# Mixer of a fused transformer kernel: compressed-block weights spread between other chunks, a third buffer for decayed tokens, exponents in steps 1 and 2, masks ahead of gates

## The chip, the cores and the metric

One core of one Trainium2 chip. The metric is the device time of one execution in microseconds (us). The kernel before took 1908.52 us (median of 3 runs, 1904.62 to 1910.46).

## The reference, cut to what matters

Two transformer blocks on 256 tokens of width 1024, in float32. The first block is FFN, hybrid mixer, FFN; the second holds four more FFNs and two other attention mixers. The change touches the hybrid mixer alone:

```python
o_nsa = nsa_group(...)     # 8 heads: window, selected and compressed-block attention
o_hg  = hgrn2_group(...)   # 4 heads of a gated linear recurrence, chunks of 64 tokens
return jnp.concatenate([o_nsa, o_hg], -1) @ w_out

# hgrn2: f = lb + (1-lb)*sigmoid(z); b = cumsum(log f) in a chunk
decay = jnp.exp(jnp.where(tril, b[t] - b[s], NEG))
a = einsum('bhtd,bhtsd,bhsd->bhts', qc, decay, kc)
o = einsum('bhts,bhsv->bhtv', a, vc) + (qc * exp(b)) @ state
```

The compressed blocks of the attention part are windows of 32 tokens (15 of them), put through a hidden layer of 256 (weights `cmp_w1`, GELU) and a second layer, once for keys and once for values.

## The kernel before, in words

**Weights.** All weights come from memory in 128-partition chunks of up to 1.5 MB, in the order of use, through four buffers `w_raw`; chunk i goes into the buffer that chunk i-4 leaves. SyncE (SP) issues the loads in order, each behind a wait until chunk i-4 is used (`load`, L1815). A chunk is split for exact products at the fast matmul rate: ScalarE (ACT) makes `w_hi` (L319), VectorE (DVE) makes `w_lo` = raw - hi (L326), each with two buffers; TensorE (PE) makes three products per tile (L354 feature-major, L363 token-major). The `cmp_w1` chunks are the exception: they are multiplied raw (L775) and leave their buffer when PE has used them (`hid_tile`).

**Mixer, first part** (`pe_mixer`, L752). PE works through `nsa_a`, `nsa_v`, `hg_g` (2 chunks), `hg_fq` (4), `hg_v` (2), `cmp_w1` (4), `nsa_b`, `nsa_c`. ACT and DVE turn the results into gates, queries, keys and the logarithms of the forget gates; DVE scans them into `b_sum` (L1093).

**Decayed tokens.** Per hgrn head, eight "levels" of exponents are written into a buffer `decayed` of 128 x 2048: DVE's `away(h)` writes differences of `b_sum` (L1106 to L1116), ACT's `decays(h)` takes their exponential (L942), GpSimd's (POOL) `left(h)` multiplies half of it by `hk` (L1229), DVE's `right(h)` the other half by `hq` (L1124). There are two such buffers, lent from `gains` and `logs`. Heads 0 and 1 are made before the steps, heads 2 and 3 inside steps 2 to 5.

**Steps.** Then come STEPS = 8 steps (and two in which the last outputs drain), a loop of k on every engine. Step k takes attention head k and unit k of the recurrence (head k//2, token block k%2). In it, by engine:

- PE: `scores(k)` (L802 to L807), `values(k-2)` (L819 to L821), `level_products(k)` (L831 to L838), `turn_output(k-2)` (L843), `outputs(k-1)` (L850), `turn_weights(k-1)` (L862 to L866).
- DVE: `mean_square(k-2)` (L1139), `weights(k)` (L1154 to L1164: bias and maximum), `gate_output(k-2)` (L1146), `value_lo(k-2)` (L1170), `gated_weights(k)` (L1183 to L1190: waits for ACT's exponentials and scales them), `mask_levels(k)` (L1199), `output_lo(k-2)` (L1177), and in steps 2 and 4 `away`, in 3 and 5 `right`.
- ACT: `weights(k)` (L973, exponentials of the softmax), `value_hi(k-2)` (L980), `copy_cross` (L991), `output_hi(k-2)` (L985), `keep_output(k-1)` (L997, L999), `copy_weights(k-1)` (L1005 to L1007), and `decays` in 2 and 4.
- POOL: the root for `gate_output(k-2)` (L1245), `sum_levels(k)` (L1236 to L1238, sums the masked levels), and `left` in 2 and 4.

The order on each engine is written out by hand, and every engine works its list in order. After the steps the output projection (`w_out1` x2, `w_out2`) runs, then the next FFN. The first half of `w_out1` is split before the steps.

## Time and profile before

| what | value |
|---|---|
| median of 3 runs | 1908.52 us (1904.62 to 1910.46) |
| the profiled execution | 1906.41 us, its span 1905.1 us |
| PE busy | 1772.9 us, 93% of the span |
| DVE, ACT, POOL busy | 55%, 46%, 6% |
| the chain of work that ended last, by engine | PE 82%, DVE 9%, ACT 5% |
| mean granted TensorE clock | 0.962 of full |
| the mixer | about 207 to 442 us of the span |

The span runs from the first to the last instruction; times below are us from its start. A granted clock of 1.00 is 2.4 GHz on TensorE, 0.50 is 1.2 GHz. A row of the timeline reads: start, duration from first to last end, engine, line, operation, output<-inputs, count, and in brackets the idle time before it and what ended it.

### The profile page before, as it was taken

How to read it: one execution, taken by the hardware profiler on the slowest of the kernel's cores; microseconds unless marked ns; L12 is line 12 of the kernel's file. 1: busy time of each engine (PE TensorE's matmuls, PEld its weight loads, DVE VectorE, ACT ScalarE, POOL GpSimd, SP SyncE). 2: the span in 40 equal slices, each digit the busy share in tenths (PEclk: the TensorE clock that was granted, in tenths of full speed). 3: DMA queues.
4: the chain of work that ended last, by engine and by line, in shares of the span. 5: the costliest groups of instructions: out<-in, count | busy, mean ns of one | idle time of the engine just before them, and what ended most of it. 6: DMA issues, size and time to landing. Idle time of an engine off the chain costs nothing.

```text
span 1905.1 us, 28247 instructions
## 1 busy us (share of the span) xinstructions
PE 1772.9 (93%) x11932; PEld 1616.4 (85%) x11932; DVE 1048.9 (55%) x1709; ACT 878.7 (46%) x1507; POOL 107.3 (6%) x147
## 2 busy tenths in 40 slices
PE   7999987789999999989989998899998998999985
PEld 7999987568999999988779998799997776899984
DVE  5555566745455554555755545465556554554555
ACT  5444445435444444445644444454443554444443
POOL 0000003311000000002110000100000000100000
PEclk9999998779999999999999999999998998999998
DMA  8554353004554555434336454255543232555521
GB/s 333 191 187 169 133 194 150 23 33 161 193 185 181 188 181 185 166 133 178 144 121 227 172 195 168 98 195 191 178 185 127 92 114 78 190 187 193 187 90 44
DMA packets 31965, 301.80 MB, mean 158 GB/s; under 512 B 3792, under 2 KB 4320, under 8 KB 5856
## 3 DMA queue, kind: packets, MB, share of 16 engines
q1 hardware_dynamic: 31840, 300.01, 43.1%
q8 instruction: 94, 1.54, 0.3%
q14 instruction: 31, 0.25, 0.0%
HBM read 298.93 MB, written 1.06 MB: 157 GB/s over the span
## 4 chain that ended last, share of the span: by engine, by line
PE 82%; DVE 9%; ACT 5%; issue 2%; POOL 2%; DMA 1%; SPq 0%; DVEq 0%; ACTq 0%; POOLq 0%
PE bank L354 45%; PE bank L363 29%; DVE w_lo L326 2%; ACT w_hi L319 2%; DVE x L584 1%; DVE x L608 1%; PE bank L1276 1%; POOL rstd L668 1%; PE bank L375 1%; DVE xT_lo L617 1%; PE bank L398 1%; PE bank L384 1%; PE bank L399 1%; PE bank L1583 1%; ACT mix_s L973 0%
## 5 line engine op out<-in xcount | busy, mean ns | idle before, releaser
L326 DVE TENSOR_TENSOR w_lo<-w_raw,w_hi 128x1024 fp32r<-128x1024 f32 (+5 forms) x545 | 610.1, 1172 | 398.0 <-ACT w_hi L319 397.4
L319 ACT ACTIVATE w_hi<-w_raw 128x1024 fp32r<-128x1024 f32 (+5 forms) x561 | 525.0, 996 | 290.7 <-PE bank L363 264.2
L354 PE MATMUL bank<-xT_hi,w_hi 128*128 128x256 f32 x2264 | 642.9, 284 | 10.4 <-DVE w_lo L326 9.8
L354 PE MATMUL bank<-xT_hi,w_lo 128*128 128x256 f32 x2264 | 641.5, 283 | 0.0
L354 PE MATMUL bank<-xT_lo,w_hi 128*128 128x256 f32 x2264 | 641.4, 283 | 0.0
L354 PEld LDWEIGHTS bank<-xT_hi,w_hi 128*128 128x128 f32 x2264 | 434.9, 192 | 21.0 <-DVE w_lo L326 11.3
L354 PEld LDWEIGHTS bank<-xT_lo,w_hi 128*128 128x128 f32 x2264 | 434.9, 192 | 4.7
L354 PEld LDWEIGHTS bank<-xT_hi,w_lo 128*128 128x128 f32 x2264 | 434.9, 192 | 0.0
L363 PE MATMUL bank<-w_hi,hT_hi 128*128 128x512 f32 x528 | 207.0, 392 | 0.0
L363 PE MATMUL bank<-w_hi,hT_lo 128*128 128x512 f32 x528 | 206.9, 392 | 0.0
L542 ACT ACTIVATE ff_silu<-bank 128x256 f32<-128x256 f32 x132 | 50.7, 384 | 336.7 <-PE bank L354 334.4
L363 PE MATMUL bank<-w_lo,hT_hi 128*128 128x512 f32 x528 | 205.4, 389 | 0.0
L637 DVE TENSOR_TENSOR ff_silu<-ff_silu,bank 128x256 f32<-128x256 f32 x132 | 55.6, 421 | 185.8 <-ACT ff_silu L542 185.2
L363 PEld LDWEIGHTS bank<-w_lo,hT_hi 128*128 128x128 f32 x528 | 99.2, 188 | 21.7
L363 PEld LDWEIGHTS bank<-w_hi,hT_hi 128*128 128x128 f32 x528 | 99.6, 189 | 17.3
L363 PEld LDWEIGHTS bank<-w_hi,hT_lo 128*128 128x128 f32 x528 | 99.6, 189 | 15.9
L363 PE MATMUL bank<-w_hi,xT_hi 128*128 128x256 f32 (+3 forms) x272 | 93.3, 343 | 9.9 <-DVE xT_lo L617 4.8
L668 POOL TENSOR_TENSOR rstd<-rstd,minus_half 128x1 f32<-128x1 f32 x24 | 21.5, 895 | 1264.2 <-DVE rstd L574 1264.2
L363 PE MATMUL bank<-w_hi,xT_lo 128*128 128x256 f32 (+3 forms) x272 | 92.4, 340 | 0.0
L363 PE MATMUL bank<-w_lo,xT_hi 128*128 128x256 f32 (+3 forms) x272 | 92.0, 338 | 0.0
L639 DVE TENSOR_TENSOR hT_lo<-ff_silu,hT_hi 128x256 fp32r<-128x256 f32 x132 | 56.0, 425 | 63.8 <-ACT hT_hi L546 63.8
L546 ACT ACTIVATE hT_hi<-ff_silu 128x256 fp32r<-128x256 f32 x132 | 55.1, 417 | 64.3 <-DVE ff_silu L637 64.3
(314 smaller groups left out, 2014.4 us busy)
## 6 DMA issues: line engine op xcount, KB each, us to landing
w_raw<-in_ffn_a SPq DMA_DIRECT2D x22, 1536.0 KB, 6.5
w_raw<-in_ffn_b SPq DMA_DIRECT2D x22, 1536.0 KB, 6.4
w_raw<-in_ffn_c SPq DMA_DIRECT2D x22, 1536.0 KB, 6.4
w_raw<-in_ffn_d SPq DMA_DIRECT2D x22, 1536.0 KB, 6.4
w_raw<-in_ffn_e SPq DMA_DIRECT2D x22, 1536.0 KB, 6.4
w_raw<-in_ffn_f SPq DMA_DIRECT2D x22, 1536.0 KB, 6.4
gains<-in_gains SPq DMA_DIRECT2D x11, 1024.0 KB, 4.6
w_raw<-in_mla_up SPq DMA_DIRECT2D x8, 1280.0 KB, 5.7
```

The lines of the kernel that those rows point to most:

```text
L319: nc.scalar.activation(w_hi[c.pair][:, a:b], raw[c.slot][:, a:b], ACTF.Copy).then_inc(w_hi_made, 1)
L326: nc.vector.tensor_tensor(w_lo[c.pair][:, a:b], raw[c.slot][:, a:b], w_hi[c.pair][:, a:b].bitcast(F32), ALU.subtract).then_inc(w_lo_made, 1)
L354: ins = nc.tensor.matmul(o, w[:, c], a[:, k, :], start=(n == 0), stop=(n == last))
L363: ins = nc.tensor.matmul(o, a(k)[:, tok_of(b)], w[:, c], start=(first_k and n == 0), stop=(last_k and n == 3 * len(ks) - 1))
L375: nc.tensor.matmul(psum[7][:, 0:P], ident, ident, start=True, stop=True)
L384: ins = nc.tensor.transpose(bank[:, i * P:(i + 1) * P], src[:, b, (k0 + i) * P:(k0 + i + 1) * P], ident)
L398: nc.tensor.matmul(o, hi[:, c], xT_hi[:, k, :], start=(k == 0), stop=False)
L542: nc.scalar.activation(sig[s][:, :], gate[:, 0:SEQ], ACTF.Silu).then_inc(silu_made, 1)
L546: nc.scalar.activation(hT_hi[s][:, :], sig[s][:, :], ACTF.Copy).then_inc(h_hi_made, 1)
L637: nc.vector.tensor_tensor(sig[s][:, :], sig[s][:, :], up[:, SEQ:2 * SEQ], ALU.mult).then_inc(h_made, 1)
L639: nc.vector.tensor_tensor(hT_lo[s][:, :], sig[s][:, :], hT_hi[s][:, :].bitcast(F32), ALU.subtract).then_inc(h_lo_made, 1)
L668: nc.gpsimd.tensor_tensor(rstd[:, b:b + 1], rstd[:, b:b + 1], expo[:, 0:1], ALU.pow).then_inc(rooted, 1)
```

## The change

1. Stream: the four `cmp_w1` chunks now come ahead of `hg_fq` 2, `hg_fq` 3, `hg_v` 0 and `hg_v` 1, and PE multiplies each right there. Both halves of the hidden layer go to one PSUM bank; the other tiles take other banks. ACT copies `part` and splits `nsa_b` before the two logarithms; DVE splits `nsa_b` ahead of the gain product and the scan.
2. A third buffer for decayed tokens: head 2 uses the `w_raw` buffer of `w_out1` 0 (split before), head 3 uses `gains` again. Loads of `ffn_b` 1 and of the gains wait accordingly.
3. `right(1)` moves into step 0, the split of `w_out1` 0 into steps 0 (ACT) and 1 (DVE), `away(2)` and `away(3)` into steps 1 and 2, their exponents (`decays`) too, `left(2)` and `left(3)` into steps 2 and 3; `right(2)`, `right(3)` stay in 3 and 5. `decays(1)` stands ahead of the copies of the compressed keys (`k_cmp`).
4. In DVE's step `mask_levels(k)` stands ahead of `gated_weights(k)`; in ACT's step `value_hi(k-2)` stands ahead of `weights(k)`.

```diff
+    behind_cmp = {("hg_fq", 2): 0, ("hg_fq", 3): 1, ("hg_v", 0): 2, ("hg_v", 1): 3}
-    for name in ("ffn_a", "nsa_a", "nsa_v", "hg_g", "hg_fq", "hg_v", "cmp_w1", "nsa_b", "nsa_c", "w_out1", "w_out2",
+    for name in ("ffn_a", "nsa_a", "nsa_v", "hg_g", "hg_fq", "hg_v", "nsa_b", "nsa_c", "w_out1", "w_out2",
...
+        for i in range(t[name].shape[0]):
+            if (name, i) in behind_cmp:
+                take("cmp_w1", behind_cmp[name, i])
+            take(name, i)
...
         decayed = [a.rearrange("p (l s) -> p l s", l=LEVELS) for a in (
-            gains[:, 0:LEVELS * SEQ], logs[:, :, :, :].rearrange("p a h s -> p (a h s)"))]
+            gains_lent, logs[:, :, :, :].rearrange("p a h s -> p (a h s)"),
+            raw[chunks[first["w_out1"]].slot][:, 0:LEVELS * SEQ], gains_lent)]
...
+            compressed(0)
+            pe_features(place["hg_fq", 2], [(bank(6), (gate_made_hg, 2)), (bank(7), (gate_made_hg, 3))], mix_tile)
+            compressed(1)
+            pe_features(place["hg_fq", 3], [(bank(0), (gate_made_hg, 4)), (bank(2), (fk_sig_made, 1))], mix_tile)
+            compressed(2)
+            pe_tokens(place["hg_v", 0], SEQ, [(bank(3), (q_made, 1)), (bank(4), (fk_sig_made, 2))], mix_tile)
+            compressed(3)
+            pe_tokens(place["hg_v", 1], SEQ, [(bank(5), (q_made, 2)), (bank(6), (fk_sig_made, 3))], mix_tile)
...
             (act_mixer)
+            act.wait_ge(hid_tile, 4)
+            for kv in range(2):
+                nc.scalar.activation(part[kv], psum[1][:, kv * CMP_HID:(kv + 1) * CMP_HID], ACTF.Copy).then_inc(part_made, 1)
+            act_split(first["nsa_b"])
             flat = lambda a: a.rearrange("p h s -> p (h s)")
             act.wait_ge(floor_made, 1)
...
             copy_values(0)
-            act_split(first["nsa_b"])
-            decays(0)
             copy_values(1)
             act_split(first["nsa_c"])
-            decays(1)
+            decays(0)
...
-            act_split(first["w_out1"])
+            decays(1)
             act.wait_ge(cmp_made, 1)
...
             for k in range(STEPS + 2):
+                if k >= 2:
+                    value_hi(k - 2)
                 if k < STEPS:
                     weights(k)
-                if k >= 2:
-                    value_hi(k - 2)
...
-                if k in (2, 4):
-                    decays(1 + k // 2)
+                if k == 0:
+                    act_split(first["w_out1"])
+                if k in (1, 2):
+                    decays(k + 1)
...
             (dve_mixer)
             away(0)
-            dve_split(first["nsa_b"])
+            dve_split(first["nsa_c"])
+            right(0)
             away(1)
-            right(0)
-            dve_split(first["nsa_c"])
-            right(1)
-            dve_split(first["w_out1"])
...
+                if k == 0:
+                    right(1)
+                elif k == 1:
+                    dve_split(first["w_out1"])
+                    away(2)
+                elif k == 2:
+                    away(3)
+                elif k in (3, 5):
+                    right(2 + k // 5)
                 if k < STEPS:
+                    mask_levels(k)
                     gated_weights(k)
-                    mask_levels(k)
                 if k >= 2:
                     output_lo(k - 2)
-                if k in (2, 4):
-                    away(1 + k // 2)
-                if k in (3, 5):
-                    right(1 + k // 2)
...
             (pool_mixer)
-                if k in (2, 4):
-                    left(1 + k // 2)
+                if k in (2, 3):
+                    left(k)
...
             (sp_program)
-            loads(RAW_SLOTS, first["ffn_b"] + 2)
+            loads(RAW_SLOTS, first["ffn_b"] + 1)
 
             sp.wait_ge(gram_made, 12)
             sp.wait_ge(cross_made, 3)
+            loads(first["ffn_b"] + 1, first["ffn_b"] + 2)
+            sp.wait_ge(gram_made, 16)
+            sp.wait_ge(cross_made, 4)
             load_gains(2)
```

## Rows read from the trace of the kernel before

**Rows 1.** Stretches: us, busy per engine (instructions), granted clock, DMA share, GB/s.

```profile
223.00:280.00 57.00, 56.96 (x506) 55.14 (x504) 36.09 (x64) 29.90 (x54) 0.00 (x0) 1.00 0.51 179
280.00:288.60 8.60, 0.00 (x1) 0.03 (x1) 4.31 (x9) 5.02 (x4) 0.00 (x0) 0.64 1.00 421
...
402.80:417.80 15.00, 10.87 (x35) 6.50 (x35) 2.40 (x9) 3.47 (x11) 3.44 (x5) 0.58 0.00 1
```

**Rows 2.** The chain of waits in order of time, end of the first part.

```profile
277.43 6.10 DMA w_raw<-in_nsa_b
283.55 1.49 ACT w_hi L319
285.07 3.44 DVE w_lo L326 x2
288.60 10.63 PE bank L354 x72
```

**Rows 3.** Timeline of ACT: the second logarithm, and an exponent of a head.

```profile
272.51 1.04 ACT L931 ACTIVATE mix_logs<-mix_logs 128x1024 f32<-128x1024 f32 x1
...
293.04 1.92 ACT L942 ACTIVATE mix_logs<-mix_logs 128x2048 f32<-128x2048 f32 x1 [0.97 <-DVE mix_logs L1116]
```

**Rows 4.** Timeline of DVE: scan, end of `away(0)`, `right(0)` beside POOL, `right(1)` alone.

```profile
274.85 2.44 DVE L1093 TENSOR_TENSOR_SCAN mix_b<-const,mix_logs 128x256 f32<-128x256 f32 x4
...
280.52 0.25 DVE L1116 TENSOR_SCALAR gains<-mix_b 128x64 f32<-128x64 f32 x1
...
292.93 3.77 DVE L1124 TENSOR_TENSOR gains<-gains,xn 128x128 f32<-128x128 f32 x8
...
299.43 2.48 DVE L1124 TENSOR_TENSOR mix_logs<-mix_logs,xn 128x128 f32<-128x128 f32 x8
```

**Rows 5.** Timeline of DVE: where steps 0, 2, 6 and 7 begin, and 7 ends.

```profile
312.76 0.69 DVE L1154 SCALAR_TENSOR_TENSOR mix_s<-const,bank 128x512 f32<-128x512 f32 x1 [1.64 <-PE bank L807]
...
328.31 0.69 DVE L1154 SCALAR_TENSOR_TENSOR mix_s<-const,bank 128x512 f32<-128x512 f32 x1 [0.28 <-PE bank L807]
...
382.71 0.67 DVE L1154 SCALAR_TENSOR_TENSOR mix_s<-const,bank 128x512 f32<-128x512 f32 x1
...
394.03 0.69 DVE L1154 SCALAR_TENSOR_TENSOR mix_s<-const,bank 128x512 f32<-128x512 f32 x1 [2.30 <-PE bank L807]
...
402.77 0.14 DVE L1139 TENSOR_SCALAR mix_rms<-mix_squares 128x1 f32<-128x1 f32 x1
```

**Rows 6.** Timeline of PE: first scores of steps 0, 6 and 7.

```profile
309.41 1.80 PE L802 MATMUL bank<-mix_keys,mix_q 64*128 64x256 f32 x4 [2.62 <-ACT mix_v_cmp L965]
...
378.66 2.07 PE L802 MATMUL bank<-mix_keys,mix_q 64*128 64x256 f32 x4
...
392.06 1.13 PE L802 MATMUL bank<-mix_keys,mix_q 64*128 64x256 f32 x4
```

**Rows 7.** Timeline of DVE, step 0: `gated_weights` from its start to the mask behind it.

```profile
317.53 0.19 DVE L1183 RECIPROCAL mix_sums<-mix_sums 128x6 f32<-128x6 f32 x1 [2.51 <-ACT mix_sc L973]
...
319.13 1.28 DVE L1199 TENSOR_TENSOR lent_x<-bank,const 128x512 f32<-128x512 f32 x2
```

**Rows 8.** Timeline of POOL, step 2: first and last sum of `sum_levels`.

```profile
336.64 1.44 POOL L1236 TENSOR_TENSOR lent_x<-lent_x 128x512 f32<-128x512 f32 x1 [5.46 <-DVE lent_x L1199]
...
339.10 0.59 POOL L1238 TENSOR_TENSOR ff_silu<-lent_x 128x128 f32<-128x128 f32 x1
```

**Rows 9.** Timeline of DVE, step 2: one operation of `away`, beside POOL and alone.

```profile
336.87 1.36 DVE L1108 TENSOR_TENSOR gains<-mix_b 128x128 f32<-128x128 f32 x1
...
340.36 0.28 DVE L1108 TENSOR_TENSOR gains<-mix_b 128x128 f32<-128x128 f32 x1
```

**Rows 10.** Timeline of POOL, step 3: `left(2)`.

```profile
344.00 3.45 POOL L1229 TENSOR_TENSOR gains<-gains,xn 128x128 f32<-128x128 f32 x8 [4.31 <-ACT gains L942]
```

**Rows 11.** Timeline of DVE and of PE, step 3: who waits behind `left(2)`.

```profile
347.99 0.35 DVE L1146 SCALAR_TENSOR_TENSOR mix_o_gated<-mix_o_gated,mix_rms,mix_hg_gate 128x128 f32<-128x128 f32 x1 [3.79 <-POOL mix_rms L1245]
...
348.94 0.45 PE L843 MATMUL bank<-const,mix_o_gated 128*128 128x128 f32 x1 [7.29 <-DVE mix_oT_lo L1170]
```

More of the change, by code:

```diff
@@ L168, in weight_stream @@
                  "ffn_f", "ple1_p", "ple1_g1", "ple1_g2"):
-        first[name] = len(chunks)
-        n, _, cols = t[name].shape
-        for i in range(n):
-            split = cuts(name, i, cols) if name != "cmp_w1" else ()
-            by_pool = 4 if i == 0 and name in ("ffn_b", "ffn_d", "ffn_e", "ffn_f") else 0
-            chunks.append(Chunk(name, t[name][i, :, :], cols, split, by_pool))
+        for i in range(t[name].shape[0]):
+            if (name, i) in behind_cmp:
+                take("cmp_w1", behind_cmp[name, i])
+            take(name, i)
     landed = [0] * RAW_SLOTS
@@ L206, in weight_stream @@
         c.hi_at[j], c.lo_at[j], c.pool_at[j] = hi, lo, pool
-    return chunks, first
+    return chunks, first, place
 FFN = ("ffn_a", "ffn_b", "ffn_c", "ffn_d", "ffn_e", "ffn_f")
@@ L736, in build @@
         LEVELS = 8
+        gains_lent = gains[:, 0:LEVELS * SEQ]
         decayed = [a.rearrange("p (l s) -> p l s", l=LEVELS) for a in (
-            gains[:, 0:LEVELS * SEQ], logs[:, :, :, :].rearrange("p a h s -> p (a h s)"))]
+            gains_lent, logs[:, :, :, :].rearrange("p a h s -> p (a h s)"),
+            raw[chunks[first["w_out1"]].slot][:, 0:LEVELS * SEQ], gains_lent)]
+        fq_and_v = [place["hg_fq", h] for h in range(HG)] + [place["hg_v", 0], place["hg_v", 1]]
         units = [(h, b) for h in range(HG) for b in range(TB)]
@@ L778, in pe_mixer, with compressed @@
-            pe_features(first["nsa_b"], [(bank(7), (fk_sig_made, 4)), (bank(0), (q_made, 4)), (bank(1), (hv_copied, 1))], mix_tile)
+            def compressed(n):
+                kv, half = n // 2, n % 2
+                c = chunks[place["cmp_w1", n]]
+                pe.wait_ge(pads_zeroed, 1)
+                pe.wait_ge(nsa_copied, 2)
+                pe.wait_ge(blocks_made, 4 * kv + 4)
+                pe.wait_ge(w_landed[c.slot], c.landed)
+                for j in range(LP // 2):
+                    lp = half * LP // 2 + j
+                    rows = slice(32 * (lp % 4), 32 * (lp % 4) + N_CMP)
+                    ins = nc.tensor.matmul(psum[1][rows, kv * CMP_HID:(kv + 1) * CMP_HID], blocks[:, kv, lp, :],
+                                           raw[c.slot][:, j * CMP_HID:(j + 1) * CMP_HID], start=(lp < 4), stop=(lp >= LP - 4))
+                ins.then_inc(hid_tile, 1)
@@ L909, in act_mixer @@
                 nc.scalar.activation(vals[:, b, :], psum[3 + b][:, 0:VSW], ACTF.Copy).then_inc(nsa_copied, 1)
-            act_split(first["hg_fq"])
+            act_split(place["hg_fq", 0])
             act.wait_ge(nsa_copied, 5)
@@ L944, in act_mixer @@
             copy_values(0)
-            act_split(first["nsa_b"])
-            decays(0)
             copy_values(1)
             act_split(first["nsa_c"])
-            decays(1)
-            for kv in range(2):
-                act.wait_ge(hid_tile, 2 * kv + 2)
-                nc.scalar.activation(part[kv], psum[5 + kv][:, 0:CMP_HID], ACTF.Copy).then_inc(part_made, 1)
+            decays(0)
             act.wait_ge(mix_tile, 22)
@@ L1057, in dve_mixer @@
             dve_split(first["hg_g"] + 1)
-            dve_split(first["hg_fq"])
+            dve_split(place["hg_fq", 0])
             cmp_gates = gates[:, :, :].rearrange("p b (h three) -> p b h three", three=3)[:, :, :, 0]
@@ L1084, in dve_mixer @@
             nc.vector.tensor_scalar(f, f, LN_RANGE, None, ALU.max).then_inc(floor_made, 1)
+            dve_split(first["nsa_b"])
             by_head = hg[:, :, :].rearrange("p b (h v) -> p (b h) v", v=P)
@@ L1819, in load @@
                 if left >= 0:
-                    name = chunks[left].name
-                    at = left - first[name]
-                    if name == "cmp_w1":
-                        sp.wait_ge(hid_tile, at + 1)
+                    if chunks[left].name == "cmp_w1":
+                        sp.wait_ge(hid_tile, chunks[left].at + 1)
                     else:
```

88 lines of the change are left out of this document (41 added, 47 removed).

## The prediction

> **What bounds the kernel now.** I read the busy time by stretch first. In the first part of the mixer PE is busy all the time at full clock [rows 1]: there the number of matmuls sets the time. Then PE stands still from 280.0 to 288.6. The chain of waits says why [rows 2]: the `nsa_b` load is issued at 277.4, when PE has used the first `cmp_w1` chunk, and takes 6.1 us; ACT's first half of the split (1.5) and DVE's two (3.4) follow. In steps 0 to 7 the starts of DVE's `weights` are the marks [rows 5]: 15.6 us for steps 0 and 1, 54.4 for steps 2 to 5 (four of 13.6), 11.3 for step 6, 8.7 for step 7. Two things hold the long steps. DVE waits 3.8 us for POOL's root, which stands behind `left(2)` [rows 10, 11]. And TensorE's clock falls to 1.2 GHz after its long waits (7.3 us [rows 11]): a whole step of PE, scores to scores, then lasts 13.4 us (378.7 to 392.1), with the same scores at 2.07 us against 1.13 at 2.4 GHz [rows 6]. From 402.8 to 417.8 the last outputs drain, mostly at the lower clock (0.58 granted) [rows 1].
>
> **The change, part by part.** All times are laid on the profiled execution.
>
> *First part.* Each `cmp_w1` chunk costs PE the same wherever it stands (3.7 us for the four, 276.3 to 280.0, by the end of the first part [rows 1, 2]). `nsa_b` now goes into the buffer of the third, used after `hg_fq` 3. PE's order then ends: `hg_fq` 3 at 266.7, third `cmp_w1` 267.7, `hg_v` 0 273.4, fourth 274.4, `hg_v` 1 280.1. So `nsa_b` is issued at 267.7, lands by 274 and stops being on the path. On SP each `hg_fq`/`hg_v` load now stands behind the wait for the `cmp_w1` ahead of it: pairs of 2 MB, issued at 254.4 (`hg_v` 0) and 261.1 (`hg_v` 1). At the 421 GB/s that the engines reached when loads were queued [rows 1] a pair takes 5 us, at the single load's pace [rows 2] 8; they are needed, split, at 267.7 and 274.4, so both fit. ACT waits for the fourth `cmp_w1` (274.4), copies `part` (0.6), splits `nsa_b` (2.9) to 278.0; DVE follows to 280.1. PE goes on at once: the 8.6 us hole closes, and `nsa_b` runs at full clock to 288.9 (it took 10.6 us [rows 2], half as much again as a two-tile chunk of 5.8, so 8.6; 1.9 of it was the clock).
>
> *What is late next.* Behind ACT's wait for `hid_tile` and the split stand the two logarithms: they end at 281.3 instead of 273.5 [rows 3]. DVE's gain product ends then too; sum 1.2, scan 2.4, `away(0)` 3.5 [rows 4] give 288.6 instead of 280.8. The recurrence is 7.8 us later than before, and it is what binds: split of `nsa_c` to 290.8, `right(0)` beside `left(0)` 3.8 [rows 4], `away(1)` to 298.5. `decays(1)` (1.9 [rows 3]) now stands ahead of the `k_cmp` copies: 300.4, copies 300.8, first scores 300.95. PE has been ready since 297.6; that place in ACT's queue costs 3.3 us. The scores began at 309.4 [rows 6]: **8.5 us gained**. `weights(0)` begins at 304.3 for 312.8.
>
> *A step of DVE alone.* `weights` 2.25 (312.76 to the 2.51 us wait that ends at 317.53 [rows 5, 7]), `gate_output` and `value_lo` 0.7, mask 1.2, `gated_weights` 1.6 [rows 7], `output_lo` 0.2: 6.0. Before, 2.5 us of waiting for exponentials came on top [rows 7]; the mask and the earlier `value_hi` now fill that.
>
> *What the new order brings in.* POOL sums the levels right behind the mask, and `gated_weights` now lies beside those sums. Beside the first sum (1.44 us) one DVE operation with two SBUF inputs took 1.36 us instead of its 0.28 [rows 8, 9]: it stood until POOL's ended. The three sums lasted from 336.6 to 339.7. `gated_weights` (six such operations) was never beside POOL in this trace, so I bound it: 1.6 if nothing collides, 1.6 + 3.05 = 4.65 if DVE gets in only when POOL is done. DVE gets a turn between the sums as in [rows 9], so I take 3.7. The Trainium skill (GPSIMD Engine Reference, Specifications) says that POOL's SBUF interfaces are shared with VectorE for instructions with two SBUF inputs. By it `weights`, whose second input is PSUM, is untouched, and `gated_weights` is not. By that rule the masks ahead of the gates give back most of what they win.
>
> *Steps 0 and 1.* Step 0: 2.2 + `right(1)` 2.5 + 1.2 + 3.7 = 9.6. Step 1: 2.2 + split of `w_out1` 3.4 (as large as `nsa_b`'s [rows 2]) + `away(2)` 3.4 + 1.2 + 3.7 = 13.9. Together 23.5 for 15.6: **7.9 lost**. ACT's half of the split hides behind DVE's step 0. PE waits about 5 us in step 1 (314 to 318.9), so I take it at 1.2 GHz until about 334.
>
> *Steps 2 to 5.* Step 2: 6.0 + `away(3)` 3.4 (no POOL beside it) + 2.1 = 11.5. Step 3: POOL sums until 339.0, then `left(2)` 3.45 [rows 10], then the root: DVE waits 1.6; 6.0 + 2.1 + 1.6 + `right(2)` 2.5 = 12.1. Step 4 the same wait behind `left(3)`: 9.7, but PE, at the lower clock after a 3.7 us wait in step 3, gives the levels 0.6 late: 10.3. Step 5: 6.0 + 2.1 + 2.4 = 10.5. Together 44.4 for 54.4: **10.0 gained**.
>
> *Steps 6 and 7.* 8.0 for 11.3, as PE is no longer in its slow stretch: **3.3 gained**. Step 7 8.8 for 8.7. The tail and the projection are taken as before (15.0 and 24.2 us): they hang on PE and on the same chain. Loads of `ffn_b` 1 and the gains wait for levels of steps 5 and 7 (365 and 383) and are needed after 420: nothing. The third buffer itself costs nothing: DVE split its chunk just before.
>
> **Sum:** -8.5 + 7.9 - 10.0 - 3.3 + 0.1 = -13.8. The profiled execution took 1906.4, so 1892.6; the median of the runs shown is 2.1 higher, so 1894.7. I take **1894**.
>
> **The rivals.**
>
> *A. No collision* (chance 0.15). `gated_weights` keeps its 1.6. Each step loses 2.1 less, but in steps without extra work the exponentials (ready 4.8 us into the step) or PE then bind, so I count 1.5 for each of eight: 12 more, **1881**. For it: no row shows this very operation beside POOL. Against: [rows 8, 9].
>
> *B. The gain stays upstream* (0.10). PE at the lower clock in steps 4 to 7, too: each then lasts the 13.4 us of [rows 6]. Against my 10.3, 10.5, 8.0, 8.8 that is +3.1, +2.9, +5.4 and up to +4.6 less what the clock's return takes off: about +9 to +12, **1904** to 1906, no difference that can be measured. Against: full work brought the clock back in the stretch of [rows 6] within one step.
>
> *C. Slower* (0.05). PE's clock decides all steps. If scores(0) to scores(7) take seven times 13.4 = 93.8 us, scores(7) start at 394.8 instead of 392.1 [rows 6], run 3.3 instead of 1.9 us, and values and levels of step 7, at the lower clock, add 4: 8 us late, **1916**. It decides from 13.0 us a step (the 8.5 us upstream, over seven steps, on top of the 11.8 of now). For it: PE's waits of 3 to 5 us in steps 1, 3 and 6 are new or stay.
>
> *D. The loads don't keep up* (0.05). A pair of 2 MB lands after 9 us instead of 5 to 8, and PE waits 2 to 3 us at `hg_v` 0 or 1: **1897**.
>
> **How the numbers follow.** My own case has 0.65. A measurement of this kernel tells 0.3%, 5.7 us, from no change: faster is below 1902.8, slower above 1914.2. Faster: my case, A, D and a small part of B: 0.86. Same: 0.09. Slower: C, 0.05. The range runs from A, 1881, to just short of B's times, 1902: the ends of `gated_weights` (1.6 and 4.65; the upper one adds up to 7.6, 1901.6) lie inside.
>
> **What would show it.** The wait of PE for `nsa_b` gone (right under 1 us, wrong over 3). First scores near 301; over 304 and the recurrence is later than I say. `gated_weights` from its reciprocal to its last product at 3 to 4.6 us and POOL's first sum beside it; at 1.6 it is A. Step 1 the longest of the early ones, 13 to 15 us. DVE's wait for the root in steps 3 and 4, 1 to 3 us, none in 5. Granted clock of steps 2 to 7 above 0.75; at 0.55 it is B or C. Start of the projection at 402 to 406 for 417.8. The times from there to the end must be unchanged; if they aren't, the sum is wrong by what I left out.

## The result, and the profile after

The changed kernel takes **1891.62 us** (median of 4 runs, 1889.33 to 1893.77); the kernel before took 1907.38 beside it. Ratio 0.9912, 95% interval 0.9895 to 0.993: faster by 15.8 us. I had said 1894, in 1881 to 1902. The profiled execution is the quickest of the four (1889.33, span 1888.0).

Stretches of the changed kernel; columns as in [rows 1]:

```profile
223.00:280.00 57.00, 57.00 (x499) 54.14 (x498) 32.57 (x47) 32.01 (x56) 0.00 (x0) 1.00 0.65 240
280.00:301.00 21.00, 16.91 (x142) 16.58 (x142) 16.11 (x52) 13.45 (x20) 8.97 (x11) 1.00 0.49 193
...
336.40:348.80 12.40, 11.56 (x51) 9.20 (x51) 9.96 (x30) 5.07 (x21) 6.95 (x13) 0.63 0.00 1
...
372.00:380.00 8.00, 6.81 (x33) 4.66 (x32) 6.18 (x18) 2.48 (x11) 3.32 (x4) 0.76 0.00 0
...
389.00:404.00 15.00, 11.08 (x54) 7.93 (x54) 5.36 (x8) 5.82 (x12) 0.55 (x1) 1.00 0.07 14
```

PE is busy through 280 and beyond: the second row of [rows 1], 8.6 us without a matmul, has no counterpart. The third row is step 3, mostly at the lower clock. The last row is where the drain ends and the projection begins, at full clock; before, the drain had 0.58. What binds the end of the first part now, by the chain of waits (start, duration, what):

```profile
274.63 2.75 ACT w_hi L327 x2
...
277.40 1.28 ACT L953
...
282.00 2.45 DVE mix_b L1114 x4
...
287.92 2.28 DVE w_lo L334 x2
...
290.29 6.00 PE bank L362 x48
...
296.71 1.28 ACT L965
...
298.01 1.91 ACT mix_logs L965
...
300.29 1.25 PE bank L821 x4
```

Against [rows 2], the load of `nsa_b` is no longer in it. The chain runs through ACT's half of that split, the logarithms (1.28 is the table load ahead of them), the sum, the scan, `away(0)` and the split of `nsa_c`, and at its end through two things on ACT of which I had priced one: the exponent of head 1, and not the load of a function table (1.28) ahead of it.

Where DVE's steps begin and end, and two places inside them (timeline of DVE, for [rows 5, 11]):

```profile
303.10 0.69 DVE L1177 SCALAR_TENSOR_TENSOR mix_s<-const,bank 128x512 f32<-128x512 f32 x1 [6.79 <-PE bank L826]
...
339.70 0.35 DVE L1169 SCALAR_TENSOR_TENSOR mix_o_gated<-mix_o_gated,mix_rms,mix_hg_gate 128x128 f32<-128x128 f32 x1 [1.02 <-POOL mix_rms L1274]
...
381.54 0.69 DVE L1222 TENSOR_TENSOR lent_x<-bank,const 128x512 f32<-128x512 f32 x1 [1.24 <-PE bank L850]
...
387.37 0.14 DVE L1162 TENSOR_SCALAR mix_rms<-mix_squares 128x1 f32<-128x1 f32 x1
```

The wait for POOL's root is 1.02 us (step 3; the same again in step 4) for 3.79 in [rows 11]. Step 7 (from 375.72) became longer: its masks wait for levels that PE makes at the lower clock (0.76 in the window 372 to 380).

`gated_weights` of step 0, timeline of DVE:

```profile
306.88 1.29 DVE L1222 TENSOR_TENSOR lent_x<-bank,const 128x512 f32<-128x512 f32 x2
308.08 0.19 DVE L1206 RECIPROCAL mix_sums<-mix_sums 128x6 f32<-128x6 f32 x1
308.30 1.38 DVE L1210 TENSOR_TENSOR mix_wgt<-mix_sums,mix_gates 128x2 f32<-128x2 f32 x3
309.71 1.76 DVE L1213 TENSOR_TENSOR mix_s<-mix_s,mix_wgt 128x512 f32<-128x512 f32 x2
```

and beside it on POOL:

```profile
308.25 1.27 POOL L1265 TENSOR_TENSOR lent_x<-lent_x 128x512 f32<-128x512 f32 x1 [4.81 <-DVE lent_x L1222]
309.59 0.74 POOL L1266 TENSOR_TENSOR lent_x<-lent_x 128x256 f32<-128x256 f32 x1
```

Three products of 128x2 elements last 1.38 us: as long as POOL's first sum. From the reciprocal's start to the end of the last product it is 3.5 us (308.08 to 311.57), 3.4 to the next operation, where [rows 7] had 1.6.

Where every kernel of this study has its steps, by the start of `weights(k)` on DVE (the last column is the projection's first matmul on PE, us of each span):

| kernel | 0 | 1 | 2 | 3 | 4 | 5 | 6 | 7 | projection | median us |
|---|---|---|---|---|---|---|---|---|---|---|
| before | 312.8 | 320.3 | 328.3 | 342.0 | 355.5 | 369.2 | 382.7 | 394.0 | 417.8 | 1907.4 |
| **changed** | 303.1 | 311.5 | 325.2 | 336.4 | 348.8 | 357.5 | 367.2 | 375.7 | 397.8 | 1891.6 |
| stream_only | 314.4 | 322.0 | 330.0 | 343.6 | 357.2 | 370.9 | 384.4 | 393.6 | 413.9 | 1908.3 |
| old_stream | 312.3 | 320.7 | 334.4 | 345.7 | 357.4 | 366.1 | 377.4 | 386.0 | 408.9 | 1898.1 |
| two_buffers | 303.1 | 311.5 | 321.7 | 332.6 | 345.9 | 356.9 | 370.2 | 381.7 | 403.1 | 1898.3 |
| gates_first | 303.2 | 310.8 | 322.9 | 333.2 | 345.3 | 356.4 | 364.7 | 372.6 | 392.5 | 1887.0 |
| sums_behind | 304.1 | 310.6 | 322.8 | 333.1 | 345.3 | 356.3 | 364.5 | 371.8 | 389.5 | 1882.9 |
| kcmp_first | 299.8 | 309.8 | 323.5 | 334.7 | 347.1 | 355.8 | 367.5 | 376.0 | 399.0 | 1889.0 |
| warm | 304.3 | 312.6 | 326.4 | 337.6 | 348.6 | 357.4 | 367.8 | 376.8 | 400.9 | 1890.1 |
| all3 | 303.5 | 311.7 | 328.8 | 338.0 | 350.2 | 361.1 | 371.4 | 380.6 | 405.7 | 1891.1 |
| sums_kcmp | 301.5 | 309.6 | 321.8 | 332.1 | 344.7 | 355.2 | 363.5 | 370.8 | 390.0 | 1880.7 |
| root_first | 300.0 | 308.2 | 320.3 | 330.7 | 341.1 | 349.0 | 357.8 | 365.3 | 383.0 | **1877.7** |

In the mixer the changed kernel gains 20.0 us up to the projection (417.79 to 397.78), and the projection itself lasts 22.68 for 24.23. Against the projection's start in `before_again`, a second profile of the kernel before, it is 18.2. By the spans the whole kernel gains only 17.1. The rest of the program is the same code; it moved by a few us from one execution to the next (see `before_again`), so I take nothing from it.

### The profile page after: what moved, and what is told of

Its sections match the earlier page's. It is cut to its first block, busy times and chain, and to the rows that moved or that the text cites. A ratio compares the mean times of both kernels' runs of the same rounds, so it can differ in the third digit from the quotient of the medians.

```text
span 1888.0 us, 28249 instructions
## 1 busy us (share of the span) xinstructions
PE 1765.6 (94%) x11932; PEld 1610.1 (85%) x11932; DVE 1052.7 (56%) x1709; ACT 877.5 (46%) x1507; POOL 109.5 (6%) x147
## 4 chain that ended last, share of the span: by engine, by line
PE 82%; DVE 10%; ACT 4%; issue 2%; POOL 1%; DMA 0%; SPq 0%; DVEq 0%; ACTq 0%
PE bank L362 45%; PE bank L371 29%; DVE w_lo L334 2%; ACT w_hi L327 2%; DVE x L592 1%; DVE x L616 1%; PE bank L1305 1%; POOL rstd L676 1%; DVE xT_lo L625 1%; PE bank L406 1%; PE bank L383 1%; PE bank L392 1%; PE bank L407 1%; PE bank L1612 1%; DVE mix_wgt L1210 1%
## 5 line engine op out<-in xcount | busy, mean ns | idle before, releaser
L362 PEld LDWEIGHTS bank<-xT_hi,w_hi 128*128 128x128 f32 x2264 | 434.2, 192 | 13.8 <-issue 5.9
L371 PEld LDWEIGHTS bank<-w_lo,hT_hi 128*128 128x128 f32 x528 | 99.3, 188 | 21.6
```

The costliest lines, as they stand in the source:

```text
L362: ins = nc.tensor.matmul(o, w[:, c], a[:, k, :], start=(n == 0), stop=(n == last))
L371: ins = nc.tensor.matmul(o, a(k)[:, tok_of(b)], w[:, c], start=(first_k and n == 0), stop=(last_k and n == 3 * len(ks) - 1))
```

## The experiments

Each was timed beside the kernel before, on the same chip as it; `before_again` is a single execution. Unless said otherwise the edit is made in the changed kernel. No kernel leaves a part of the computation out.

### Is each part worth something? stream_only, old_stream, two_buffers

**stream_only** keeps part 1 alone: buffers, places of `away`, `right`, `left`, exponents and the orders of a step are those of before.

```diff
             away(0)
-            dve_split(first["nsa_c"])
-            right(0)
             away(1)
+            right(0)
+            dve_split(first["nsa_c"])
+            right(1)
+            dve_split(first["w_out1"])
...
+            decays(0)
             copy_values(1)
             act_split(first["nsa_c"])
-            decays(0)
+            decays(1)
```

> The kernel after with the parts 2, 3 and 4 undone: only the order of the weight chunks and what hangs on it (PSUM banks, nsa_b split ahead of the logarithms) is changed against the kernel before. My theory: PE's wait for nsa_b goes, but the recurrence (logarithms, scan, both away, right(0), split of nsa_c, then ACT's split of w_out1 ahead of the k_cmp copies) is then the bound, and the first scores come only about 1 to 3 us earlier than before (309.4): 1904 to 1907, within 0.3% of the kernel before. Rival (the 8.6 us hole is a gain of its own): 1898 to 1900, first scores near 301.

Measured: 1908.3 us (1904.5 to 1912.14), ratio 1.0005, interval 0.9992 to 1.0017. Within 0.3% of before, as my theory said, though above its 1904 to 1907: the first scores come at 310.8, 1.4 us later than before and not 1 to 3 earlier. The rival (1898 to 1900) fell. Timeline of PE in stream_only:

```profile
300.02 0.55 PE L362 MATMUL bank<-xT_hi,w_hi 128*128 128x256 f32 x1 [9.40 <-DVE w_lo L334]
```

`nsa_b` comes in time, and PE then stands 9.4 us for the split of `nsa_c`, which DVE does last behind the recurrence. The hole of [rows 2] (8.6 us) has moved by one chunk. It is a mechanism that the prediction described ("The recurrence is 7.8 us later than before, and it is what binds"), seen here with DVE's old order behind it.

**old_stream** undoes part 1 and keeps the other three: the four chunks stand together ahead of `nsa_b`, which ACT and DVE split where before did.

```diff
-            if (name, i) in behind_cmp:
-                take("cmp_w1", behind_cmp[name, i])
+            if name == "nsa_b":
+                for n in range(4):
+                    take("cmp_w1", n)
             take(name, i)
```

> The kernel after with part 1 undone: the cmp_w1 chunks stand ahead of nsa_b again, so PE waits for the nsa_b load as before; third buffer, exponents in steps 1 and 2, masks ahead of gates stay. My theory after stream_only (part 1 alone: 1908.3, no gain): the parts need each other. Without part 1 the first scores come at about 306 instead of 300.3 (w_out1's split no longer stands ahead of the k_cmp copies), the steps run as in after: 1896 to 1900. Rival (the gain is in the steps alone, part 1 worth nothing): 1890 to 1893. Other rival (part 1 worth the 8.6 us here): 1900 or more.

Measured: 1898.12 us (1895.08 to 1909.53), ratio 0.9954 (0.9938 to 0.997); inside the theory's 1896 to 1900, though the first scores come at 308.7 and not at 306. The hole is back in front of `nsa_b`; timeline of PE in old_stream:

```profile
287.60 0.55 PE L363 MATMUL bank<-xT_hi,w_hi 128*128 128x256 f32 x1 [8.55 <-DVE w_lo L335]
```

So part 1 is worth 6.5 us by the medians (1898.1 against 1891.6; 11.1 by the projection's start) with the others, and nothing alone. Old_stream also puts the split of `nsa_c` back behind `right(0)` and `away(1)`, where stream_only has it too. PE's wait in stream_only points at that split as what part 1 needs beside it; the split was not moved alone, so this is argued and not shown.

**two_buffers** gives back the two buffers and the late heads: `away`, exponent and `left` of heads 2 and 3 in steps 2 and 4, behind the step's other work, `right` in 3 and 5.

```diff
-            raw[chunks[first["w_out1"]].slot][:, 0:LEVELS * SEQ], gains_lent)]
+            gains_lent, logs[:, :, :, :].rearrange("p a h s -> p (a h s)"))]
...
-                if k in (1, 2):
-                    decays(k + 1)
+                if k in (2, 4):
+                    decays(1 + k // 2)
...
-                if k in (2, 3):
-                    left(k)
+                if k in (2, 4):
+                    left(1 + k // 2)
```

> The changed kernel with two buffers for decayed tokens again: away, exponent and left of heads 2 and 3 in steps 2 and 4, behind the step's other work, right in 3 and 5, all as before; the stream, the places of right(1) and of w_out1's split, and the order of masks and gates stay as in the changed kernel. Theory: the third buffer and the earlier exponents are worth the stall behind left(2) and left(3): the root comes 3 to 4 us late in steps 3 and 5, where it is 1.0 in the changed kernel, while step 1 gets shorter by away(2) (3.4 us). weights(1) to weights(2) about 10.3, steps 2 to 5 together about 48 to 50 instead of 42; 1895 to 1900. Rival: DVE has the same work in either order and the waits overlap with PE's own slow stretches, so the third buffer is worth under 3 us: 1888 to 1894. Another rival: the stall comes whole in both steps and PE's clock falls with it: 1901 or more.

Measured: 1898.34 us (1897.01 to 1902.34), ratio 0.9951 (0.9938 to 0.9963). The theory held. Steps 2 to 5 last 48.6 us (321.7 to 370.2; 42.0 in the changed kernel). Timeline of POOL, step 3 of two_buffers:

```profile
334.63 3.45 POOL L1253 TENSOR_TENSOR gains<-gains,xn 128x128 f32<-128x128 f32 x8 [5.96 <-ACT gains L965]
338.04 0.55 POOL L1269 TENSOR_TENSOR mix_rms<-mix_rms,minus_half 128x1 f32<-128x1 f32 x1
```

and of DVE, steps 3 and 5:

```profile
338.62 0.35 DVE L1165 SCALAR_TENSOR_TENSOR mix_o_gated<-mix_o_gated,mix_rms,mix_hg_gate 128x128 f32<-128x128 f32 x1 [3.79 <-POOL mix_rms L1269]
...
362.92 0.35 DVE L1165 SCALAR_TENSOR_TENSOR mix_o_gated<-mix_o_gated,mix_rms,mix_hg_gate 128x128 f32<-128x128 f32 x1 [3.79 <-POOL mix_rms L1269]
```

`left(2)` waits 5.96 us for its exponent, and DVE then 3.79 for the root: the stall of [rows 10, 11], to the hundredth, back in both steps. The third buffer, with the earlier heads that it allows, is worth 6.7 us by the medians (5.3 by the projection's start).

### The order within a step: gates_first, sums_behind

**gates_first** puts `gated_weights` ahead of `mask_levels` on DVE again, and nothing else.

```diff
                 if k < STEPS:
-                    mask_levels(k)
                     gated_weights(k)
+                    mask_levels(k)
```

> The kernel after with gated_weights(k) ahead of mask_levels(k) again on DVE, nothing else. My theory: the sums on POOL no longer collide with the products (gated_weights back from 3.4 to 1.6 us), but DVE waits for the exponentials again, so the two cancel: within 3 us of the kernel after (1891.6). Rival (the order of masks and gates is worth its full 1.3 us a step): 8 to 12 us slower than after, 1900 to 1904. Other rival (the collision outweighs): up to 6 us faster.

Measured: 1887.01 us (1883.38 to 1892.74), ratio 0.9894 (0.9876 to 0.9912): 4.6 us faster by the medians than with the change's order. The two intervals still overlap (0.9895 to 0.9912), but the trace says the same: the projection starts 5.3 us earlier (392.45 for 397.78). That is the rival in which the collision outweighs what the masks hide. The exponents were not much to hide: DVE waits for them 0 to 1.27 us in this kernel, not the 2.51 of [rows 7]; in the early steps `right(1)`, `away` and the split now fill that time.

By step the picture is less simple. Steps 0, 1, 2 and 5 are 0.8 to 1.5 us shorter. In steps 3 and 4 DVE waits 4.24 us for the root instead of 1.02, since POOL's sums begin later; step 4 is 2.4 us longer. The largest single gain is step 7 with 3.4 us (8.3 for 11.7), and there PE's granted clock is 0.98 where the changed kernel has 0.71. Without step 7 the gain up to the projection would be about 2 us (an estimate from these rows), which is the theory's "within 3 us".

**sums_behind** leaves the masks first and makes POOL's sums wait for `gated_weights`.

```diff
                 pool.wait_ge(masked_made, 2 * u + 2)
+                pool.wait_ge(p_made, u + 1)
                 pool.wait_ge(hg_out_made, u - 1)
```

> The kernel after, where POOL's sum_levels(k) also waits until gated_weights(k) is done (p_made). Same work, no collision. My theory: gated_weights takes 1.6 us instead of 3.4 in each step, DVE's steps shorten where DVE is the bound; in steps 2 and 3 the left multiplications and the root behind the sums are not later than now. 4 to 10 us faster than after: 1882 to 1888. Rival (the collision costs nothing on the path, since exponentials or PE bind the step anyway): 1890 to 1893.

Measured: 1882.87 us (1878.08 to 1890.46), ratio 0.9875 (0.9856 to 0.9895): 8.7 us faster than the changed kernel. A wait was added, and the kernel became faster. Step 0 on DVE:

```profile
309.03 0.18 DVE L1206 RECIPROCAL mix_sums<-mix_sums 128x6 f32<-128x6 f32 x1
309.24 0.30 DVE L1210 TENSOR_TENSOR mix_wgt<-mix_sums,mix_gates 128x2 f32<-128x2 f32 x3
309.58 1.03 DVE L1213 TENSOR_TENSOR mix_s<-mix_s,mix_wgt 128x512 f32<-128x512 f32 x2
```

and the first sum on POOL:

```profile
310.85 1.27 POOL L1266 TENSOR_TENSOR lent_x<-lent_x 128x512 f32<-128x512 f32 x1 [5.76 <-DVE mix_sc L1213]
```

with `weights(1)` beside it on DVE:

```profile
310.62 0.68 DVE L1177 SCALAR_TENSOR_TENSOR mix_s<-const,bank 128x512 f32<-128x512 f32 x1
```

The same three products that took 1.38 us beside POOL take 0.30, and `gated_weights` is back at 1.6. Steps 0 to 2 are shorter by 1.8, 1.5 and 0.9 us, steps 5 and 6 by 1.5 and 1.2. Step 4 is longer (10.9 for 8.7): DVE waits 4.30 us for the root there and in step 3, since POOL now does sums, `left` and root one after the other and starts later.

The largest gain is again step 7, 6.7 us for 11.7, with the granted clock at 1.00 for 0.71. The same order of step 7 as in the changed kernel lasts 8.5 us in two_buffers, at a granted clock of 1.00. So some 3 us of the 8.7 came with PE's clock in step 7 and not from the products themselves (an estimate: 11.7 less 8.5). The clock of step 7 is 0.68 to 0.71 in the changed kernel, kcmp_first and old_stream, and 0.98 or more in gates_first, sums_behind, sums_kcmp and root_first; whether the order brings this about was not tried.

### The end of the first part, and the clock: kcmp_first, warm, all3

**kcmp_first** moves the exponent of head 1 behind the copies of the compressed keys.

```diff
-            decays(1)
             act.wait_ge(cmp_made, 1)
             nc.scalar.activation(k_cmp[:, :], psum[3][:, P:P + GROUPS * NB], ACTF.Copy)
...
+            decays(1)
```

> The kernel after, where ACT copies k_cmp and v_cmp ahead of decays(1) instead of behind it. My theory: decays(1) stands 3.2 us in the way of the first scores (300.3), which then come near 297.5, 1 to 3 us gained in all, as right(1) in step 0 now waits a little for decays(1): 1889 to 1891. Rival (step 0 is bound by the recurrence, so nothing moves): 1891.6 within 1 us.

Measured: 1888.97 us (1883.67 to 1892.76), ratio 0.9902 (0.9884 to 0.992). The first scores come at 297.9 for 300.3, as expected; but step 0 is then 9.9 us for 8.4, since `right(1)` now lies beside `left(1)` and takes 3.25 us instead of 1.70, and the projection starts no earlier (399.0 for 397.8). Its median is 2.6 us lower than the changed kernel's, but the intervals overlap, and the trace does not show the gain behind step 1. I count it as small or nothing.

**warm** keeps PE busy where it waits: matmuls of 128x128 into bank 3, which nothing reads before it is written anew (30 in step 1 ahead of `turn_weights(0)`, 8 to 20 ahead of the values of steps 3 to 8; each is two instructions in the trace).

```diff
+            def warm_step(count):
+                for _ in range(count):
+                    nc.tensor.matmul(psum[3][:, 0:P], ident, ident, start=True, stop=True)
...
                 if k >= 2:
+                    pe.wait_ge(pT_made, 3 * (k - 2) + 3)
+                    warm_step({3: 20, 4: 8, 5: 8, 6: 8, 7: 8, 8: 16}.get(k, 0))
                     values(k - 2)
...
                     outputs(k - 1)
+                    warm_step({1: 30}.get(k, 0))
                     turn_weights(k - 1)
```

> The kernel after with extra 128x128 matmuls into an unused PSUM region where PE waits in steps 1 and 3 to 8 (30, 20, then 8 to 16 of them), so that TensorE's clock stays at 2.4 GHz; they leave the output alone. My theory: in after PE at 1.2 GHz makes DVE wait for the levels in steps 3 and 7 and slows outputs; 4 to 8 us less: 1884 to 1888, granted clock in the steps 0.95 or more for 0.82. Rival (DVE is the bound, clock off the path): 1890 to 1893.

Measured: 1890.14 us (1886.54 to 1892.09), ratio 0.9902 (0.9885 to 0.9919). The time is that of the rival (1890 to 1893) and not of the theory (1884 to 1888). The stretch 300 to 400 in warm:

```profile
300.00:400.00 100.00, 86.58 (x604) 74.43 (x604) 77.11 (x213) 46.25 (x170) 37.19 (x56) 0.97 0.07 27
```

and in the changed kernel:

```profile
300.00:400.00 100.00, 77.09 (x418) 61.80 (x419) 78.83 (x215) 47.36 (x171) 37.13 (x56) 0.83 0.07 27
```

The granted clock rises from 0.83 to 0.97. That the time did not follow is not because the clock is off the path. Steps 3 and 7 and the drain in warm:

```profile
337.60:348.60 11.00, 9.63 (x67) 8.02 (x67) 9.78 (x29) 4.91 (x21) 6.86 (x13) 1.00 0.01 1
...
376.80:386.00 9.20, 7.21 (x52) 5.76 (x51) 7.52 (x20) 4.91 (x21) 3.33 (x4) 0.99 0.31 113
386.00:400.90 14.90, 10.97 (x65) 8.54 (x63) 2.43 (x9) 3.49 (x11) 1.10 (x2) 0.89 0.00 1
```

and what PE does at the start of that drain:

```profile
385.38 5.47 PE L892 MATMUL bank<-const 128*128 128x128 f32 x32 [1.20 <-ACT lent_x L1032]
390.77 0.65 PE L838 MATMUL bank<-lent_x,mix_vals 128*64 128x256 f32 x2
```

Step 3 lasts 11.0 us for 12.3 and step 7 9.2 for 11.7: there the theory had put DVE's waits for PE, and there the clock gave 3.8 us. Steps 5 and 6 became 0.7 and 0.5 longer, but the eight steps together are 2.5 us shorter (81.8 for 84.3). The drain then lasts 14.8 us for 10.4: the values of head 6 stand behind the 16 dummies of step 8 until 390.8. So the dummies took back what the clock had won. Without those of step 8 the kernel would come to about 1885.7 (an estimate: 1890.1 less the 4.4 us of the drain), inside the theory's range; that kernel was not run. The first scores were also 1.9 us later than in the changed kernel (302.2), ahead of any dummy.

**all3** is sums_behind, kcmp_first and warm together.

> The kernel after with three edits together: POOL's sums wait until gated_weights is done, k_cmp copied ahead of decays(1), and the extra matmuls of warm. If the three gains add (8.7 from the sums, 2.6 from k_cmp, 4 to 8 from the clock): 1872 to 1877. If the sums' gain was mostly the better clock it happened to bring, less: 1878 to 1881.

Measured: 1891.07 us (1888.56 to 1897.63), ratio 0.992 (0.9901 to 0.9938). A miss by over 10 us: two edits that gained and a third that had cost no time alone came to nothing together. Timeline of DVE, start of step 2 of all3:

```profile
328.82 0.69 DVE L1184 SCALAR_TENSOR_TENSOR mix_s<-const,bank 128x512 f32<-128x512 f32 x1 [4.87 <-PE bank L826]
```

and of PE ahead of it:

```profile
316.56 9.49 PE L892 MATMUL bank<-const 128*128 128x128 f32 x60
```

PE waits for the later sum ahead of `outputs(0)`, and only then come the 30 dummy matmuls, in front of `turn_weights(0)` and `scores(2)`. In warm they began at 312.7 and took 6.9 us, most of it in a wait (4.8 us in the changed kernel) and without making step 2 later; here the wait had moved ahead of them, and they stood in the way. The drain, with its 16 dummies, lasts 16.4 us, for 12.6 in sums_kcmp below.

### What follows: sums_kcmp, root_first

**sums_kcmp** is all3 without the dummies (the two diffs above).

> The changed kernel with two of its orders altered, as in sums_behind (POOL's sums of a step wait for gated_weights, so that the two don't lie beside each other) and kcmp_first (the copies of the compressed keys ahead of the exponent of head 1), without the dummy matmuls of warm. Theory: the third combination lost because of the 30 dummy matmuls in front of turn_weights(0); without them the two gains (8.7 and 2.6 us alone) add up in part. First scores near 298, step 0 about 9 us long (right(1) waits for the exponent), weights(1) near 309 and every later step as in sums_behind: 1878 to 1882. Rival: step 0 takes back all that kcmp_first gives (weights(1) at 310.6 as in sums_behind): 1882 to 1885. Another rival: outputs(0), late behind the later sum, holds PE in step 1 whatever the dummies do, so weights(2) comes after 325 instead of 322.8: 1886 to 1891.

Measured: 1880.7 us (1879.5 to 1883.73), ratio 0.9858 (0.9841 to 0.9875), within the theory's 1878 to 1882. That the dummies were all3's fault is shown by this pair: 10.4 us between them, and `weights(2)` at 321.8 instead of 328.8. Against sums_behind (1882.9) it is 2.2 us, with overlapping intervals: not a difference that can be counted on. What is left to take is in DVE's steps 3 and 4:

```profile
338.65 0.35 DVE L1169 SCALAR_TENSOR_TENSOR mix_o_gated<-mix_o_gated,mix_rms,mix_hg_gate 128x128 f32<-128x128 f32 x1 [4.28 <-POOL mix_rms L1275]
...
350.82 0.35 DVE L1169 SCALAR_TENSOR_TENSOR mix_o_gated<-mix_o_gated,mix_rms,mix_hg_gate 128x128 f32<-128x128 f32 x1 [3.91 <-POOL mix_rms L1275]
```

**root_first** moves `left(2)` and `left(3)` behind the root of the next step on POOL.

```diff
                     pool.wait_ge(ms_made, k - 1)
                     nc.gpsimd.tensor_tensor(rms[k % 2][:, :], rms[k % 2][:, :], expo[:, 0:1], ALU.pow).then_inc(ms_rooted, 1)
+                if k in (3, 4):
+                    left(k - 1)
                 if k < STEPS:
                     sum_levels(k)
-                if k in (2, 3):
-                    left(k)
```

> sums_kcmp (1880.7 us) with POOL's left(2) and left(3) moved behind the root of the next step: into steps 3 and 4, between root and sums. In sums_kcmp DVE waits 4.28 us (step 3) and 3.91 us (step 4) for that root, since left (3.46) stands ahead of it. Theory: DVE's waits fall to about 1 us each, 6 us less on DVE; in step 3 right(2) then lies beside left(2) and both get longer (right 1.7 to about 3.8), which gives back 2, and PE (idle only 3.05 and 1.52 us in those steps) takes some of the rest: 1875 to 1878. Rival: PE is the bound of steps 3 and 4 once DVE is quicker, so nothing comes of it: 1879 to 1882. Another rival: right(2) beside left(2) delays mask and gates of step 3 by more than the wait did: 1883 or more.

Measured: 1877.68 us (1868.98 to 1879.36), ratio 0.9827 (0.9801 to 0.9853): 31 us below before by the medians (1908.92 beside it), in the theory's 1875 to 1878, and the lowest median of all. Its interval lies below the changed kernel's and overlaps that of sums_kcmp. Timeline of DVE, steps 3 and 4 of root_first:

```profile
333.79 0.59 DVE L1169 SCALAR_TENSOR_TENSOR mix_o_gated<-mix_o_gated,mix_rms,mix_hg_gate 128x128 f32<-128x128 f32 x1 [0.86 <-POOL mix_rms L1275]
...
334.87 3.16 DVE L1150 TENSOR_TENSOR w_raw<-w_raw,xn 128x128 f32<-128x128 f32 x8
...
344.23 0.59 DVE L1169 SCALAR_TENSOR_TENSOR mix_o_gated<-mix_o_gated,mix_rms,mix_hg_gate 128x128 f32<-128x128 f32 x1 [0.86 <-POOL mix_rms L1275]
```

The waits are 0.86 us for 4.28 and 3.91; `right(2)`, now beside `left(2)`, takes 3.16 instead of the 1.70 that it took in sums_kcmp. Steps 3 and 4 last 18.4 us for 23.1.

### How much the rest moves by itself: before_again

**before_again** is the kernel before, one more profile.

> The kernel before once more, for a second profile of it. In the mixer the same as the first within 0.5 us. Open: its stage from the fifth to the sixth FFN (shared keys, MLA mixer) took 408.8 us, in all five changed kernels 412.0 to 412.3, with the same code. If that is chance (the phase of TensorE's clock), it may be 412 here; if it depends on the mixer's end, 408.8 again.

Measured: 1911.17 us, span 1909.8. Its steps start 0.2 to 0.7 us later than those of the first profile (I had said within 0.5), and its projection starts at 415.9, 1.9 us earlier. The stage of which I asked, measured from PE's last group of transpositions ahead of the fifth FFN to the same one ahead of the sixth, is 413.8 us, where the first profile has 410.3 and the changed kernel 413.5: it varies with the same code. From the projection's start to the end of the span before_again takes 1493.9 us, where the first profile of before took 1487.3, the changed kernel 1490.2, sums_behind 1487.2 and two_buffers 1492.7. Two executions of one kernel are thus 6.6 us apart behind the mixer, which is why one span against one span can't size a gain of 15.

## Why the prediction was right

The time (1894 for 1891.6), the sign and the mechanism of the first part and of the root came out; that the time came so near is partly luck, as shown below. By its own steps, each as a difference to before on the profiled executions:

| step | forecast | measured |
|---|---|---|
| first scores | -8.5 (300.95) | -9.1 (300.29) |
| steps 0, 1 | +7.9 (9.6, 13.9) | +6.5 (8.4, 13.7) |
| steps 2 to 5 | -10.0 (11.5, 12.1, 10.3, 10.5) | -12.4 (11.3, 12.3, 8.7, 9.7) |
| step 6 | -3.3 (8.0) | -2.8 (8.5) |
| step 7 | +0.1 (8.8) | +2.9 (11.7) |
| tail (15.0) | 0 | -4.6 (10.4) |
| projection (24.2) | 0 | -1.6 (22.7) |

From the first scores to `weights(0)` a higher clock gives another 0.5 (2.8 us for 3.3; the first scores take 1.25 for 1.80), which I had not counted. The eight steps last 84.3 us from `weights(0)` to the end of step 7; my eight terms add up to 84.7.

*First part: right.* `nsa_b` is issued at 267.0 (I said 267.7), PE goes from chunk to chunk without a wait until 0.98 us before `nsa_c`, and the recurrence takes over: `away(0)` ends at 287.9 (288.6), as does the split of `nsa_c` at 290.2 (290.8). The place of the exponent of head 1 ahead of the copies does cost 2.4 us of first scores (kcmp_first), which I had at 3.3. Two of its reasons were off and cancelled. `right(0)` takes 1.70 us, not 3.8, so `away(1)` is done at 296.3 and not at 298.5; and ACT is held instead by the last copy of `q` and by a table load of 1.28 that I had left out.

*The price of `right`: misread.* I took `right(1)` of [rows 4] as alone, 2.5 us, and used that for steps 0, 3 and 5. POOL was beside it; timeline of POOL in the kernel before:

```profile
295.04 5.72 POOL L1229 TENSOR_TENSOR mix_logs<-mix_logs,xn 128x128 f32<-128x128 f32 x8 [0.24 <-ACT mix_logs L942]
```

It ended at 300.8, and `right(1)` ran from 299.4 to 301.9. With POOL idle `right` takes 1.70 us in each of the three steps; that is 0.8 of the 1.2 by which step 0 came out shorter than forecast, and nearly all of the 0.8 in step 5.

*The collision: right in kind and size.* `gated_weights` takes 3.4 us (taken at 3.7; bounds 1.6 and 4.65), so rival A fell. I wrote that the masks ahead of the gates "give back most of what they win". By the medians of gates_first they cost 4.6 us, but 3.4 of the 5.3 by the rows lie in step 7 with PE's clock; the rest is near the balance that I had said. Removing the collision and keeping the masks first (sums_behind) gives 8.7 us, about 3 of them by way of that clock. What the masks could win was the 2.5 us wait for exponents of [rows 7], and with the extra work in the early steps that wait would have been 0.9 in step 0 and 1.27 or less later anyway. The Trainium skill (GPSIMD Engine Reference, Specifications) says that POOL shares its SBUF interfaces with VectorE and contends with VectorE instructions that have two SBUF inputs. The traces agree: in sums_behind `weights(1)`, whose second input is PSUM, takes 0.68 us beside POOL's first sum (310.62 and 310.85), as it does alone (0.69), while the products with two SBUF inputs take 1.38 beside it and 0.30 alone. The last section has a place where such operations are not slowed.

*Steps 2 to 5: right on the root, wrong on PE.* The waits for the root were said to be 1.6 and are 1.02, twice; two_buffers shows the stall back with the old buffers, 3.79 us twice. Step 4 was to be 10.3 because PE would give the levels late; it is 8.7, and no wait for PE stands in it. The wait stands one step earlier: in step 3, at a granted clock of 0.63, DVE waits 0.83 us for the copy behind PE's values and 0.41 for the levels, which made up for the cheaper `right` and root (12.3 for 12.1). Rivals B and C fell: steps 4 to 7 last 8.5 to 11.7 us, none 13.4, and the granted clock is 1.00 in steps 4 to 6.

*Step 7, tail and projection: the step that failed.* "The tail and the projection are taken as before (15.0 and 24.2 us): they hang on PE and on the same chain." They do hang on PE, but its clock did not stay. Step 7 and the tail in the kernel before (the second row is that of [rows 1]):

```profile
394.00:402.80 8.80, 5.67 (x39) 4.33 (x39) 5.95 (x19) 5.14 (x21) 0.19 (x2) 0.94 0.00 0
```

and in the changed one:

```profile
375.70:387.40 11.70, 8.88 (x39) 6.70 (x39) 7.76 (x21) 4.91 (x21) 3.32 (x4) 0.71 0.22 90
387.40:397.80 10.40, 6.28 (x35) 3.87 (x35) 2.40 (x9) 3.46 (x11) 1.09 (x2) 1.00 0.01 2
```

The same 39 and 35 matmuls, and the stretch at the low clock has moved from the tail (0.58 of [rows 1]) into step 7. That the length goes with the clock, other runs show. Step 7 in the changed order lasts 8.5 us in two_buffers at 1.00. The drain lasts 15.0 us at 0.58 in before, and 13.0 at 0.71 in its second profile:

```profile
402.90:415.90 13.00, 8.20 (x34) 4.66 (x34) 2.38 (x9) 3.41 (x11) 3.51 (x5) 0.71 0.00 1
```

In stream_only it is 11.6 at 0.87. In the changed kernel step 7, whose masks wait 1.24 and 0.94 us for PE, is 2.9 us longer and the tail 4.6 shorter; the two together take 22.1 for 23.8, and the projection, which starts at full clock, gives 1.6 more. How much of these 3.3 us belongs to the change stays open: before_again, without any change, already takes 21.8 for the two. From `weights(7)` to PE's first matmul behind the projection it is 47.3 us in the changed kernel, 50.5 in before and 49.7 in before_again.

*Why 1894 and 1891.6 agree better than the rows.* By the rows the mixer and projection gain 21.6 us, where my sum had 13.8: it was 7.8 short (1.1 up to `weights(0)`, 1.4 in steps 0 and 1, 2.4 in steps 2 to 5, 1.8 in step 7 and tail, 1.6 in the projection, less 0.5 in step 6). By the medians the kernel gains only 15.8. Behind the projection the first profile of before took 1463.1 us and the changed one 1467.5, which brings 21.6 down to the spans' 17.1; the profiled executions were also 1.0 and 2.3 us quicker than their medians, which brings 17.1 down to 15.8. So what my sum left out met a variation of the other sign that no edit made, and that the forecast lies 2 us from the median is luck.

**Rival D** (loads too slow) fell: PE waits for no load in the first part, and the paired loads of `cmp_w1` and `hg_v` land 5.2 and 7.3 us after their issue (medians of two each). Of the other marks, the granted clock of steps 2, 4, 5 and 6 was above 0.75 as said (0.95 and 1.00 three times); that of step 3 with 0.63 and of step 7 with 0.71 was not. The root of step 5 costs DVE nothing. The projection started earlier (397.8) than the 402 to 406 that I gave.

## What to carry to other kernels

Before placing two engines' elementwise work side by side, look at the inputs: where both had two in SBUF here, one of them was held up, and a wait that keeps them apart can be a gain (8.7 us here, about 3 of them by way of PE's clock). Put short work that another engine waits for (a root of 0.55 us) ahead of long work on the same queue, even if the long work is ready first. Closing a hole upstream can be worth nothing while the next late chunk stays late: test parts singly and in pairs, since here one was worth 0 alone and 6.5 us in company. And look at an edit stage by stage before calling it worthless: the dummy matmuls won 3.8 us in two steps and lost 4.4 in the drain.
